# The scores of a head behind the sixth half slab, and ScalarE's copies of the next head's turned keys and values behind the decays

## What is computed

```python
z = jnp.einsum('bld,dn->bln', a, w_in)
...
def step(s, inp):
    qi, ki, vi, gi = inp
    b = jnp.cumsum(gi, axis=-2)
    diff = b[..., :, None, :] - b[..., None, :, :]
    decay = jnp.exp(jnp.where(causal, diff, -jnp.inf))
    scores = jnp.einsum('bhtk,bhsk,bhtsk->bhts', qi, ki, decay)
    o = (jnp.einsum('bhts,bhsv->bhtv', scores, vi)
         + jnp.einsum('bhtk,bhkv->bhtv', qi * jnp.exp(b), s))
    b_last = b[..., -1:, :]
    s_new = (jnp.exp(b_last[..., 0, :])[..., None] * s
             + jnp.einsum('bhsk,bhsv->bhkv', ki * jnp.exp(b_last - b), vi))
    return s_new, o
```

## Time and profile before

| | us |
|---|---|
| median of 3 runs | 1767.29 |
| lowest and highest | 1758.26, 1770.8 |
| span of the profiled execution | 1764.1 |
| PE busy | 1699.0 |
| DVE busy | 1088.4 |
| ACT busy | 818.1 |
| POOL busy | 192.2 |

### The profile page before, as it was taken

The page is one execution under the profiler, slowest core; times in us unless marked ns, Lnnn a source line. Parts: engine busy times, 40 slices in busy tenths (PEclk is TensorE's granted clock), DMA queues, the critical chain, the costliest instruction groups (busy, mean ns, idle before and its releaser), DMA issues.

```text
span 1764.1 us, 37565 instructions
## 1 busy us (share of the span) xinstructions
PE 1699.0 (96%) x13820; PEld 1687.2 (96%) x13820; DVE 1088.4 (62%) x1737; ACT 818.1 (46%) x1069; POOL 192.2 (11%) x176
## 2 busy tenths in 40 slices
PE   6999999999999999999879999999999999999799
PEld 6999999999999998999869999999999999999799
DVE  6457457888887775665585544554455445555754
ACT  5475335455455444543354433443344334443554
POOL 3000001111111110005430000000000000035200
PEclk9999999999999999999999999999999999999999
DMA  6555656565565544775515555555555555555364
GB/s 224 164 192 175 203 184 195 162 207 166 172 211 177 170 159 159 233 273 182 184 59 188 189 185 168 189 185 179 184 168 189 187 177 176 175 189 188 107 209 141
DMA packets 119382, 318.51 MB, mean 181 GB/s; under 512 B 11684, under 2 KB 47268, under 8 KB 119348
## 3 DMA queue, kind: packets, MB, share of 16 engines
q1 hardware_dynamic: 117044, 315.91, 55.0%
q10 hardware_dynamic: 2304, 2.16, 0.3%
HBM read 299.94 MB, written 18.09 MB: 180 GB/s over the span
## 4 chain that ended last, share of the span: by engine, by line
PE 93%; DVE 4%; issue 1%; ACT 1%; DMA 1%; POOL 0%; SPq 0%; ACTq 0%; DVEq 0%; POOLq 0%
PE bank L260 28%; PE bank L261 28%; PE bank L262 28%; PE bank L493 2%; PE bank L480 1%; DVE room L1173 1%; DVE wlo L248 1%; PE bank L469 1%; DVE b_lo L892 1%; DVE room L1171 1%; PE bank L491 1%; PE bank L525 0%; PE bank L519 0%; PE bank L511 0%; DMA raw<-in_stream 0%
## 5 line engine op out<-in xcount | busy, mean ns | idle before, releaser
L243 ACT CAST whi<-raw 128x1024 fp32r<-128x1024 f32 x534 | 546.7, 1049 | 502.3 <-PE bank L262 424.8
L260 PE MATMUL bank<-a_hi,whi 128*128 128x264 f32 x2672 | 767.9, 287 | 0.0
L261 PE MATMUL bank<-a_lo,whi 128*128 128x264 f32 x2672 | 759.3, 284 | 0.0
L262 PE MATMUL bank<-a_hi,wlo 128*128 128x264 f32 x2672 | 758.9, 284 | 0.0
L248 DVE TENSOR_TENSOR wlo<-raw,whi 128x1024 fp32r<-128x1024 f32 x534 | 647.1, 1247 | 154.4 <-ACT whi L243 153.5
L260 PEld LDWEIGHTS bank<-a_hi,whi 128*128 128x128 f32 x2672 | 505.9, 189 | 0.5 <-issue 0.3
L261 PEld LDWEIGHTS bank<-a_lo,whi 128*128 128x128 f32 x2672 | 506.2, 189 | 0.1
L262 PEld LDWEIGHTS bank<-a_hi,wlo 128*128 128x128 f32 x2672 | 503.3, 188 | 0.0
L260 PE MATMUL bank<-b_hi,whi 128*128 128x264 f32 x1504 | 427.2, 284 | 4.3 <-DVE b_lo L1115 2.1
L261 PE MATMUL bank<-b_lo,whi 128*128 128x264 f32 x1504 | 426.1, 283 | 0.0
L262 PE MATMUL bank<-b_hi,wlo 128*128 128x264 f32 x1504 | 425.8, 283 | 0.0
(11 more groups left out here) (148 smaller groups left out, 1200.9 us busy)
## 6 DMA issues: line engine op xcount, KB each, us to landing
raw<-in_stream SPq DMA_DIRECT2D x534, 512.0 KB, 4.3
room<-in_x SPq DMA_DIRECT2D x8, 528.0 KB, 8.3
m_spill<-stage SPq DMA_DIRECT2D x32, 132.0 KB, 4.7
lev<-m_spill SPq DMA_DIRECT2D x16, 264.0 KB, 5.6
S<-in_state_hgrn SPq DMA_DIRECT2D x16, 256.0 KB, 5.1
out_new_hgrn_sample<-S SPq DMA_DIRECT2D x16, 256.0 KB, 4.7
S<-in_state_gla SPq DMA_DIRECT2D x8, 512.0 KB, 5.9
out_new_gla_sample<-S SPq DMA_DIRECT2D x8, 512.0 KB, 5.8
```

Source lines behind the costliest of these rows:

```text
L243: act.copy(whi[:, s, :], raw[:, s, :]).then_inc(hi_ready, 1)
L260: pe.matmul(out, whi[:, s, w], hi[:, k0 + k, :], start=start and k == 0, stop=False)
L261: pe.matmul(out, whi[:, s, w], lo[:, k0 + k, :], start=False, stop=False)
L262: mm = pe.matmul(out, wlo[:, s, w], hi[:, k0 + k, :], start=False, stop=stop and k == HT - 1)
```

## The change

On TensorE `scores` is called behind slab 5, where it was called in the middle of it. On ACT the three copies and their waits become a function `turned(H, D)`. It is called for head 0 ahead of the loops, and for head H + 1 at the end of head H, between `decays(H + 1)` and the wait for `o_gated`; it stood behind `slab(2)` of its own head. As the number of values copied depends on the next head's kind, head 7 gets a loop of its own on ACT. No arithmetic, no DMA and nothing on DVE, GpSimd or SyncE is changed.

```diff
@@ tensor, head @@
             slab(4)
-            slab(5, midway=lambda: scores(H, D))
+            slab(5)
+            scores(H, D)
             turn_kd(H)
             sample_out(H, D, 0)
@@ scalar @@
-        def head(H, D, more=True):
...
-            slab(2)
+        def turned(H, D):
+
             act.wait_ge(h_sem["s_turned"], now(H))
             act.wait_ge(h_sem["outer1"], before(H))
             act.copy(ks_tok[:], SC[1][0:S_ROWS, 0:P])
...
             act.wait_ge(h_sem["state_done"], before(H))
             act.copy(v_tok[:, :, 0:D * P], TP[:, 0:2 * D * P].rearrange("s (b v) -> s b v", b=2))\
                .then_inc(h_sem["v_tok_ready"], 1)
+
+        def head(H, D, next_D):
+
+            T = 4 * H + T_HEADS
+            more = next_D is not None
...
+            slab(2)
             slab(3)
             slab(4)
...
             if more:
                 slab(9)
                 decays(H + 1)
+                turned(H + 1, next_D)
             act.wait_ge(h_sem["o_gated"], now(H))
...
         decays(0)
         split(T_HEADS + 1, (T_HEADS + 1) % 2)
-        with act.Fori(0, HH) as H:
-            head(H, 1)
+        turned(0, 1)
+        with act.Fori(0, HH - 1) as H:
+            head(H, 1, 1)
+        with act.Fori(HH - 1, HH) as H:
+            head(H, 1, 2)
         with act.Fori(HH, HEADS - 1) as H:
-            head(H, 2)
+            head(H, 2, 2)
         with act.Fori(HEADS - 1, HEADS) as H:
-            head(H, 2, more=False)
+            head(H, 2, None)
```

More of the change, by code:

```diff
@@ L723, in decays @@
                .then_inc(h_sem["kd_exp"], 1)
-        def head(H, D, more=True):
+        def turned(H, D):
+            act.wait_ge(h_sem["s_turned"], now(H))
+            act.wait_ge(h_sem["outer1"], before(H))
+            act.copy(ks_tok[:], SC[1][0:S_ROWS, 0:P])
+            act.copy(vs_tok[:, 0:D * P], SC[1][0:S_ROWS, P:(1 + D) * P]).then_inc(h_sem["s_tok_ready"], 1)
+            act.wait_ge(h_sem["v_turned"], now(H))
+            act.wait_ge(h_sem["state_done"], before(H))
+            act.copy(v_tok[:, :, 0:D * P], TP[:, 0:2 * D * P].rearrange("s (b v) -> s b v", b=2))\
+               .then_inc(h_sem["v_tok_ready"], 1)
+        def head(H, D, next_D):
             T = 4 * H + T_HEADS
+            more = next_D is not None
             def slab(k):
@@ L741, in head @@
             slab(2)
[L742 to L749, removed]
             slab(3)
```

## The result

The changed kernel takes 1748.59 us (median of 4 runs, 1746.09 to 1752.75) against 1766.76 for the kernel before in the same comparison: ratio 0.9909 as estimated from all runs (95% interval 0.9881 to 0.9937; the two medians alone give 0.9897). That is 18.2 us between the medians, where 17.4 us had been worked out.

What follows compares the result with a forecast made beforehand. TensorE, busy for 96% of the span, was taken as the bound. Waits at the scores (8.8 us) and clock falls (8.6 us) gave 17.4 us off 1767.3, 1749.9, forecast 1750, range 1744 to 1764.

Steps and rivals of the forecast that it cites:

- The bound and the late party: TensorE, busy 96%, bounds the kernel; at the scores it waits 10.2 us in 11 waits for DVE's state updates.
- Worth of a wait: 8.8 us: Ahead of the scores, half a slab (1.45 us) covers waits: 3.2 us in HGRN heads, 1.2 in head 8, 4.4 in heads 9 to 11.
- Cost of a fall: 3.45 us: TensorE dropping to half clock in a GLA head: head 9's 41.23 less head 8's 37.01 less 0.77 of longer wait.
- The falls go: In GLA heads 9 to 11, 0.48 us of idle instead of 1.93 ends the half clock: 8.6 us saved.
- the first rival: Clock falls behind the scores instead, at turn_kd and narrow products in four GLA heads: 1759 us, 1755 to 1764; chance 0.30.
- The sum: 8.8 us of waits and 8.6 of clock, 17.4 us off the median 1767.3, giving 1749.9, forecast 1750.
- Falls in the median: The profiled execution has three clock falls in GLA heads; 2.5 were counted for the median, 8.6 us.
- The slower rival: Scores and narrow products together drop the clock in all 12 heads, 3.45 us each: 1791 us; chance 0.05.
- The probabilities next: At `prob_v` in HGRN heads, slack 0.8 us; if masks come later, TensorE waits 0.5 us in 8 heads: 1754; chance 0.08.
- The copies: ScalarE's three copies fit its idle time ahead of b_hi, cost and gain 0; rival, they delay b_hi: 1753, chance 0.07.

Runs made afterwards that it cites:

- a quarter of a slab: The kernel before with the scores behind the sixth of eight steps of slab 5, copies not moved: 1747.02 us, ratio 0.9902.
- both `sample_out`s together: The changed kernel with both sample_out calls directly behind turn_kd, ahead of slab 6: 1761.92 us, ratio 0.9985 to the kernel before.
- second profile: Profile of the changed kernel, unaltered, measured again in a later comparison: 1752.3 us, ratio 0.994 to the kernel before.
- the narrow products apart: The changed kernel with the first sample_out in the middle of slab 6 and the second behind it: 1744.35 us, again 1745.06; copies not moved 1744.78.
- the fastest version: Scores behind slab 5, first sample_out in the middle of slab 6 and second behind it, against the kernel before: 1744 to 1745 us.

## Why the prediction was right, and where it was off

*The bound and the late party.* TensorE's standing still ahead of the scores was the loss, and DVE's chain set its end. Right: with 1.45 us of cover 0.48 us stayed in heads 9 to 11, the number forecast, and a quarter of a slab left the 1.20 that its 0.72 us of cover should leave.

*Worth of a wait: 8.8 us.* Right in its mechanism, too small in its size. An HGRN head lost 0.68 us, not 0.46. The row's idle time begins where the last product's modelled end lies, and the stop costs more. Here are the last product of slab ahead of the scores and the first of the scores, before and after:

```profile
347.10 0.28 PE L262 MATMUL bank<-a_hi,wlo 128*128 128x264 f32 x1
347.86 0.46 PE L491 MATMUL bank<-q_b,k_b 128*128 128x128 f32 x2 [0.48 <-issue]
```

```profile
347.52 0.29 PE L262 MATMUL bank<-a_hi,wlo 128*128 128x264 f32 x1
347.64 0.39 PE L491 MATMUL bank<-q_b,k_b 128*128 128x128 f32 x2
```

From start to start it was 347.86 - 347.10 = 0.76 us before and is 347.64 - 347.52 = 0.12 now: 0.64 us went, not 0.48. The first of the scores itself is longer behind the stop, 0.46 against 0.39 us, which more than makes up the rest of the 0.68. Heads 9 to 11 still stop, so there only the 1.45 went. The heads saved 7 x 0.68 + 1.39 + 3 x 1.45 = 10.5 us in waits, not 8.8.

*Cost of a fall: 3.45 us.* Too large. Head 9 took 41.23 us and takes 36.66 with 1.45 us of wait less, so its fall cost 41.23 - 36.66 - 1.45 = 3.1 us. The comparison with head 8 had counted as clock some 0.3 us by which head 9 is longer for another cause, which stays open. Three falls come to 9.4 us, not 10.3. A single stretch of 3.4 us cost more than the 1.2 us of the forecast: 1.52 in head 10, 33.45 - 31.91 = 1.54 in an HGRN head with both `sample_out`s together.

*The falls go.* Half right. The falls behind the wait went, once 1.2 us of idle time or less stood there with the scores behind it. But a new fall stood in head 10 of the first profile (1.52 us) and three in its second profile. That is the first rival, which I gave 0.30 for all four GLA heads; it comes in some of them, and in which ones differs from execution to execution. So the forecast's "the turns of GLA heads lie 35.9 to 36.4 us apart at clock 1.00" came true in none: 35.62, 36.66 and 38.18 us, the last at 0.96.

*The sum.* Part of the closeness of 1750 to 1748.6 and 1752.3 is luck: errors that offset each other. In terms of the profiled execution the forecast had 8.8 + 10.3 = 19.1 us, and the heads did save 19.1; but by 10.5 of waits, 9.4 of falls and 0.5 in head 0, less 1.5 for the new fall, which makes 18.9. The new fall behind the heads then took the span's saving down to 17.0.

*Falls in the median.* The forecast counted 2.5 on the guess that executions differ. They do: of 51 executions of the kernel before in the later comparisons, 15 took 1756 to 1761 us at a mean granted clock of 0.990 to 0.994, 30 took 1761 to 1770 at 0.984 to 0.989, and 6 took 1777 to 1779 at 0.979 to 0.982. How many falls the median has is not shown, since one execution was profiled. At 0.991 to 0.994 the kernel before takes about 1759 us and the order with the narrow products apart 1745, so 14 us of the gain are there at like clock; the waits account for 10.5 of them, and the rest stays open.

The first rival's support was the row in which 2.0 us of scores with 1.4 us of idle did not hold the clock while slabs did. That row suggested that scores hold the clock less well than slabs do; with narrow products beside them, experiment and profile show that. The argument against it (narrow products with half a slab hold 1.00) is also true, and is just what the fastest version uses. Of the Trainium skill's rule that transposes do not count as busy ("TensorE: Matmul & The Clock Gate", Part 4) no run here shows anything for or against: with the narrow products apart the turns of kd, 0.2 us, stayed right behind the scores and the clock held, so the turns alone do not bring the falls, and whether they add to them was not tried.

*The slower rival* did not come with the change. Its mechanism did with both sample_outs together: falls reached half of the HGRN heads, for one stretch of 3.4 us each, at 1.5 us and not 3.45, and most of the gain was used up.

*The probabilities next.* Right: slack 0.8 us forecast, 0.7 in the row, and 0.46 us of wait once the scores were moved 1.2 us more. GpSimd's copies did reach DVE's last addition, and masks and additions took 0.1 us longer, inside the slack.

*The copies.* Right, at cost 0 and gain 0: the copies alone against the kernel before, and the order with the narrow products apart with and without them (within 0.3 us on one chip). The scores alone against the changed kernel is a third, from two different comparisons (0.9919 against 0.9909).

## What to carry to other kernels

When the clock falls behind a wait, cover enough of the wait to hold the clock: here a quarter of a slab brought the whole gain. Judge an order on TensorE by how wide its products are as well as by its idle time: in this kernel products one column wide did best with wide ones on both sides, not other small work. Moving work away from a place where it delays nobody, on an engine that idles in each head, gained nothing here.

## What was not expected of the hardware

The clock fell behind stretches in which the profile has TensorE busy without a gap, 3.40 of 3.40 us, with 32 or 33 products started (64-column scores and one-column products); with the narrow products between half slabs it held. The ends of products are modelled, so this busy time does not say how much of the array's time narrow products use. Idle time of 1.2 us ahead of the scores held 1.00, and 0.77 us ahead of narrow products was followed by 10.2 us at 0.50. A stop of TensorE ahead of the scores cost 0.2 us above the idle time that the profile gives it (0.68 us for 0.46). One order gave median times of 1748.6 and 1752.3 us in two comparisons, with one and three GLA heads at half clock in the profiles; what decides in which heads it falls stays open.
